# The low part of a weight a block later, a norm's squares four blocks later, its root behind the next splits

## The chip, the cores and the metric

One core of one Trainium2 chip runs the whole program. The metric is the device time of one execution in microseconds (us). TensorE (PE) does the matrix products and ScalarE (ACT), VectorE (DVE) and GpSimd (POOL) the rest. Each of them takes its instructions strictly in the order in which they were written for it, and an instruction that waits for a semaphore holds all that stand behind it. SyncE (SP) issues the transfers of the weights.

## The reference, cut to what matters

Two transformer blocks, each of depth 2, follow one another on 256 tokens of width 1024 (the first block carries 256 context tokens along in its first layer). Everything is float32. What matters here is the same everywhere: a residual stream `h`, an RMS norm of it, and a product of the normed stream with wide weights.

```python
def rms_norm(x, g, eps=NORM_EPS):              # first block
    xf = x.astype(jnp.float32)
    y = xf * lax.rsqrt(jnp.mean(xf * xf, axis=-1, keepdims=True) + eps)
    return (y * g.astype(jnp.float32)).astype(x.dtype)
...
    h_x = h_x + gt1 * y_x                                                # w_out
    f_x = modulate(rms_norm(h_x, g_ffn[l]), sh2, sc2)
    h_x = h_x + gt2 * conv_ffn(f_x, w_up[l], conv_w[l], conv_b[l], w_down[l])
    ...
    return rms_norm(h_x, g_final)
...
for layer in range(DEPTH):                     # second block
    h = h + 0.5 * _swiglu(_rmsnorm(h, ffn1_norm[layer]), ffn1_w_in[layer], ffn1_w_out[layer])
    hn = _rmsnorm(h, mix_norm[layer])
    if layer < N_A_LAYERS:
        h = h + _stick_breaking_mixer(hn, sb_w_qkv[layer], sb_w_out[layer])
    else:
        h = h + _nsa_mixer(hn, kvs, nsa_w_in[i], nsa_q_norm[i], nsa_w_out[i], cos, sin)
    h = h + 0.5 * _swiglu(_rmsnorm(h, ffn2_norm[layer]), ffn2_w_in[layer], ffn2_w_out[layer])
```

## The kernel before

**Splits.** A float32 weight is too precise for one pass of TensorE, so each is cut into a high and a low part, and each product is three matmuls: high by high, high by the activation's low part, low by high (L1207, L1208, L1209, and L1224, L1225, L1226 in the form described below). Weights come from memory in slabs of 2048 columns into three buffers RAWB. A slab is used in pieces of 1024 columns. A piece is split in two steps: ACT copies it, rounded, into WH (L1579), then DVE subtracts that from the raw weight into WL (L1899). There are four buffers for split pieces (`NW`), so the piece four ahead can be rounded only when the matmuls on a piece are done.

**Blocks.** The result is kept with its features on the 128 partitions, and a block is 128 output features. With 8 input tiles (`kt=8`) a block is 24 matmuls and uses one piece; in a down-projection chunk with 4 input tiles (`kt=4`) a block is 12 matmuls and a piece serves two blocks. Each block's bank is evacuated by DVE; in a residual stage (w_out, sb_out, nsa_out and the last chunk of each down projection) it is added into the stream H (L2098, L2128, L2132).

**The order.** One object, `Plan`, writes a single list of steps, and each engine's program walks that list and takes its own part of every step. Before a block's matmuls, `piece` calls `ahead`, which adds a `split` step for every free buffer; so the split of the piece three ahead stands on ACT and DVE just behind the evacuation of the block before.

**Norms behind a stage.** Nine residual stages feed a norm block by block (`hook`). Six use `EarlyNorm` (call them c1, f10, sb_out, f20, f11, nsa_out, in the order of time; c1, f10, f20 and f11 are last chunks of down projections, `kt=4`, the other two have `kt=8`). The norm's root is applied only to the results of the next stage, so the next stage's matmuls need just the stream itself, scaled by the gain and split: AH on ACT (L1607), AL on DVE (L1934). For the root each block is squared on ACT (L1619, L1620; the first also loads the table of Sqrt, L1613) into one of two SQ buffers, POOL adds it to an accumulator GT (L1145), TensorE sums over partitions with two matmuls (L1279, L1281), ACT takes the square root (L1628) and DVE the reciprocal (L1942). c1 is the widest: two norms in one, squares of 512 columns, and a longer chain behind the sum (L1944 to L1952). Three stages (the w_out of both layers and the last down chunk of layer 0) use `NormPlan`: there TensorE sums each block's squares and has to wait at the end for root (L1638), reciprocal (L1930), product (L1963) and the split of the normed stream (L1647, L1651, L1968).

**The next stage.** Its first two blocks run together (`mm_lead`, L1224 to L1226): for each of the eight input tiles six matmuls, 48 in all, so that tile 7 is needed last. The two sums of the norm stand behind them on TensorE.

Of the kernel before, what the change touches and what calls it, by code (L numbers as in the profile page):

```python
# [145 lines left out]
class Plan:  # L146


    def __init__(self, slabs):
        self.known, self.slabs, self.steps, self.put_off = slabs, [], [], []  # L150
        self.banks = Ring(self, 8)
        self.tmps, self.sqs, self.gts = Ring(self, 4), Ring(self, 2), Ring(self, 2)
# [70 lines left out]
    def ahead(self):  # L223
        while self.next_piece < len(self.pieces) and not self.held[self.next_piece % NW]:
# [4 lines left out]
            self.add("split", p=p)  # L229
            self.next_piece += 1  # L230

    def piece(self, s, i):
        if not self.known:
            return Piece(0, s, s.cuts[i])
        self.ahead()
        return self.pieces[s.first + i]
# [6 lines left out]
    def gemm(self, name, w, col0, ncols, T, src, ready, ev, kt=8, k0=0, width=256, fine=True, x=None, hook=None, lead=False):  # L243
        g = Gemm(name, kt, T, src, ready, ev, x)
        for c in range(0, ncols, width):
# [57 lines left out]
    def gemm_tok(self, name, w, col0, ncols, tiles, src, ready, ev, fine=True, x=None):  # L303
        g = Gemm(name, 8, 256, src, ready, ev, x)
# [288 lines left out]
    def ffn(self, name, w_up, w_down, T, ready, up, res, rx, hook):  # L593
        chunks = [[0, 1]] + [list(range(c, c + 4)) for c in range(2, 22, 4)]

        def do_up(ci):
            base = (ci % 2) * 4
# [33 lines left out]
        def do_down(ci, hook=None):  # L631
            kt = len(chunks[ci])
# [243 lines left out]
class NormPlan:  # L876
# [27 lines left out]
    def split(self, name, T, segs, W, a0=0):  # L904
        plan = self.plan
        self.sum()
        plan.mark("A" + name)
        plan.ahead()
# [16 lines left out]
class EarlyNorm:  # L925
# [4 lines left out]
    def __init__(self, plan, name, gain, first=None):  # L930
        self.plan, self.name, self.gain, self.first, self.n, self.low = plan, name, gain, first, 0, None

    def add(self, k, after):
        plan, i = self.plan, self.n
        self.n += 1
        if i == 0:
            plan.mark("A" + self.name)
            self.acc = plan.gts.take()
        q = plan.sqs.take() if i else None
        plan.add("xhi", (self.name, k), x=(after, self.gain))  # L940
# [4 lines left out]
        if self.low is not None:  # L945
            plan.add("xlow", (self.name, self.low), x=self.gain)
        self.low = k
        if i == 7:
            plan.add("xlow", (self.name, k), x=self.gain)
            b = plan.banks.take()  # L950
            plan.add("xroot", (self.name,), b=b, x=(plan.root_was, self.first))
            plan.later(1, lambda: self.sum(b, q))

    def sum(self, b, q):
        plan, name = self.plan, self.name
        plan.add("xsum", (name,), b=b, t=(self.acc, q), x=512 if self.first else 256)
        plan.sqs.give(q, ("xsum", name))
        plan.gts.give(self.acc, ("xsum", name))
        plan.banks.give(b, ("xroot", name))
# [1550 lines left out]
```

## Time and profile before

| | before |
|---|---|
| time, median of 3 runs | 2776.19 us (2770.31 to 2776.48) |
| the profiled execution: its own time | 2759.57 us |
| the profiled execution: its span | 2757.8 us |
| TensorE busy | 2562.5 us, 93% of the span |
| VectorE, ScalarE, GpSimd busy | 57%, 44%, 7% |
| mean granted TensorE clock | 0.974 of full speed |
| share of the chain that ended last | PE 77%, DVE 10%, ACT 8%, DMA 3% |

The profile shows one execution, and its time is 16.6 us under the median of the timed ones. A matmul's duration in it is modelled and overlaps the next one's; how fast TensorE goes is read from the distance between starts. A row of a timeline gives start, duration, engine, line, operation, what it writes and reads with the shapes, the count of merged instructions, and in brackets how long the engine had been idle and what ended that.

### The profile page before, as it was taken

What the parts mean: (1) busy time and instruction counts of PE and PEld (TensorE: products, weight loads), DVE (VectorE), ACT (ScalarE), POOL (GpSimd) and SP (SyncE); (2) the same over time, 40 slices, a digit from 0 to 9 for tenths busy, and PEclk for the clock granted to TensorE, in tenths of its full rate; (3) what the DMA queues carried; (4) which work ended last, traced back from release to release, by engine and by line L of the source; (5) the groups of instructions that cost most, each with busy time, mean ns of one, the idle gap of its engine ahead of it and who ended that gap; (6) DMA issues with size and microseconds to landing.
All of it is one profiled execution on the core that took longest, in us unless ns stands there. A gap on an engine that the chain in (4) does not pass through costs nothing.

```text
span 2757.8 us, 42208 instructions
## 1 busy us (share of the span) xinstructions
PE 2562.5 (93%) x17840; PEld 2259.0 (82%) x17840; DVE 1576.3 (57%) x2657; ACT 1219.8 (44%) x2025; POOL 187.4 (7%) x239
## 2 busy tenths in 40 slices
PE   5997899998999998999989989999799999988999
PEld 2875577776777776878889989998799999976999
DVE  2333234545565555364668877666566675766665
ACT  3224334424333324354556554445444553555543
POOL 0000000000000000000000011010010110025100
PEclk8998999999999999999999999999899999999999
DMA  7224432231454543233354546554265456530554
GB/s 243 67 86 131 134 105 84 67 99 61 136 169 138 168 131 129 85 115 101 122 168 155 190 145 207 185 168 130 71 201 190 153 191 199 168 126 16 169 197 140
DMA packets 337387, 382.12 MB, mean 139 GB/s; under 512 B 7408, under 2 KB 301296, under 8 KB 337200
## 3 DMA queue, kind: packets, MB, share of 16 engines
q1 hardware_dynamic: 334656, 370.37, 41.2%
q0 software_dynamic: 2544, 9.06, 1.1%
q8 instruction: 141, 2.31, 0.4%
q14 instruction: 46, 0.38, 0.0%
HBM read 378.36 MB, written 1.05 MB: 138 GB/s over the span
## 4 chain that ended last, share of the span: by engine, by line
PE 77%; DVE 10%; ACT 8%; DMA 3%; issue 2%; POOL 0%; SPq 0%; DVEq 0%; ACTq 0%; POOLq 0%
PE PS L1207 20%; PE PS L1209 19%; PE PS L1208 19%; DVE WL L1899 3%; ACT WH L1579 2%; PE PS L1242 1%; PE PS L1244 1%; PE PS L1243 1%; PE PS L1255 1%; PE PS L1224 1%; DMA RAWB<-in_w_in 1%; PE PS L1225 1%; PE PS L1226 1%; PE PS L1273 1%; PE PS L1340 1%
## 5 line engine op out<-in xcount | busy, mean ns | idle before, releaser
L1899 DVE TENSOR_TENSOR WL<-RAWB,WH 128x1024 fp32r<-128x1024 f32 (+2 forms) x613 | 734.7, 1206 | 650.5 <-ACT WH L1579 649.0
L1207 PE MATMUL PS<-AH,WH 128*128 128x256 f32 (+1 forms) x2912 | 910.7, 313 | 13.8 <-DVE WL L1899 13.8
L1209 PE MATMUL PS<-AH,WL 128*128 128x256 f32 (+1 forms) x2912 | 896.6, 308 | 0.0
L1208 PE MATMUL PS<-AL,WH 128*128 128x256 f32 (+1 forms) x2912 | 896.5, 308 | 0.0
L1579 ACT ACTIVATE WH<-RAWB 128x1024 fp32r<-128x1024 f32 (+2 forms) x613 | 625.3, 1033 | 320.0 <-PE PS L1209 167.1
L1207 PEld LDWEIGHTS PS<-AH,WH 128*128 128x128 f32 x2912 | 548.9, 189 | 70.1 <-issue 22.1
L1209 PEld LDWEIGHTS PS<-AH,WL 128*128 128x128 f32 x2912 | 548.7, 188 | 31.1
L1208 PEld LDWEIGHTS PS<-AL,WH 128*128 128x128 f32 x2912 | 548.5, 188 | 29.6 <-issue 0.5
L1207 PE MATMUL PS<-BH,WH 128*128 128x256 f32 (+1 forms) x1440 | 452.2, 314 | 0.8 <-DVE WL L1899 0.8
L1209 PE MATMUL PS<-BH,WL 128*128 128x256 f32 (+1 forms) x1440 | 439.2, 305 | 0.0
L1208 PE MATMUL PS<-BL,WH 128*128 128x256 f32 (+1 forms) x1440 | 438.5, 305 | 0.0
L1207 PEld LDWEIGHTS PS<-BH,WH 128*128 128x128 f32 x1440 | 271.5, 189 | 31.8 <-issue 13.9
L1208 PEld LDWEIGHTS PS<-BL,WH 128*128 128x128 f32 x1440 | 271.2, 188 | 15.7 <-issue 3.1
L1209 PEld LDWEIGHTS PS<-BH,WL 128*128 128x128 f32 x1440 | 271.2, 188 | 14.0
L1695 ACT ACTIVATE F<-PS,PV 128x512 f32<-128x512 f32 (+1 forms) x88 | 58.4, 666 | 136.5 <-PE PS L1209 131.0
L1224 PE MATMUL PS<-AH,WH 128*128 128x256 f32 (+1 forms) x160 | 58.0, 363 | 52.1 <-DVE AL L1968 17.2
L2105 DVE SCALAR_TENSOR_TENSOR F<-PS,PV,F 128x255 f32<-128x255 f32 x132 | 63.1, 478 | 68.6 <-ACT F L1695 68.4
L2098 DVE SCALAR_TENSOR_TENSOR H<-PS,MOD,H 128x256 f32<-128x256 f32 x168 | 72.8, 478 | 48.1 <-PE PS L1209 37.4
L1242 PE MATMUL PS<-WH,AH 128*128 128x256 f32 x352 | 99.0, 281 | 0.0
L1244 PE MATMUL PS<-WH,AL 128*128 128x256 f32 x352 | 98.1, 279 | 0.0
L1243 PE MATMUL PS<-WL,AH 128*128 128x256 f32 x352 | 98.1, 279 | 0.0
L1224 PEld LDWEIGHTS PS<-AH,WH 128*128 128x128 f32 x160 | 36.4, 227 | 60.1 <-DVE AL L1968 27.6
(314 smaller groups left out, 2827.9 us busy)
## 6 DMA issues: line engine op xcount, KB each, us to landing
RAWB<-in_f_in SPq DMA_DIRECT2D x88, 1024.0 KB, 5.2
RAWB<-in_w_in SPq DMA_DIRECT2D x52, 1024.0 KB, 5.1
RAWB<-in_w_ada SPq DMA_DIRECT2D x48, 1024.0 KB, 5.4
RAWB<-in_w_up SPq DMA_DIRECT2D x44, 1024.0 KB, 5.2
RAWB<-in_f_out SPq DMA_DIRECT2D x40, 1024.0 KB, 5.1
RAWB<-in_w_down SPq DMA_DIRECT2D x20, 1024.0 KB, 5.3
RAWB<-in_sb_qkv SPq DMA_DIRECT2D x12, 1024.0 KB, 5.4
RAWB<-in_w_out SPq DMA_DIRECT2D x8, 1024.0 KB, 5.1
```

The lines of the kernel that those rows point to most:

```text
L1207: pe.matmul(out, h, xh[:, 0:T], start=k == 0, stop=False)
L1208: pe.matmul(out, h, xl[:, 0:T], start=False, stop=False)
L1209: i = pe.matmul(out, l, xh[:, 0:T], start=False, stop=k == g.kt - 1)
L1224: pe.matmul(out[j], h, xh[:, 0:T], start=k == 0, stop=False)
L1242: pe.matmul(out, h, wh, start=k == 0, stop=False)
L1243: pe.matmul(out, h, wl, start=False, stop=False)
L1244: i = pe.matmul(out, l, wh, start=False, stop=k == 7)
L1579: act.activation(c.part("WH", p), c.raw(p.slab)[:, k0:k1, c0:c1], ACT.Copy).then_inc(up("hi", ("hi", p.p)), 1)
L1695: act.activation(c.wide(s.t, g), b[:, 0:T], ACT.Identity, bias=c.sm(f"conv_b{l}", n, 1), scale=c.sm(f"conv_w{l}", 44 + n, 1)).then_inc(up( ...
L1899: dve.tensor_tensor(c.part("WL", p), c.raw(p.slab)[:, k0:k1, c0:c1], c.part("WH", p).bitcast(F32), ALU.subtract).then_inc(up("lo", ("lo", ...
L2098: t = stt(x, b[:, q * 256:q * 256 + 256], c.mod(l, part, n, q), x, ALU.mult, ALU.add)
L2105: stt(x[:, a + 1:e], b[:, a:e - 1], c.sm(f"conv_w{l}", n, 1), x[:, a + 1:e], ALU.mult, ALU.add).then_inc(up("vec", ("upb", g.name, n, q)), 1)
```

## The change

Four things move; nothing is computed that was not computed before.

- The step `split` becomes two, `split_hi` for ACT and `split_lo` for DVE. In a stage with a hook (`lag` is set) the low part of a piece is ordered at the next call of `ahead`, a block or a pair of blocks later, unless the piece is needed at once. Everywhere else both stand together as before.
- In `EarlyNorm` the square of block i is ordered with block i+4, and the last ones follow the last block's low part.
- There the root (`xroot`) is ordered behind the sum, one tick into the next stage, and so behind the splits which that stage's first `ahead` adds. Its bank is taken there too.
- `NormPlan` itself is unchanged, but its stages set `lag`.

```diff
@@ Plan
     def ahead(self):
+
+        self.low_parts()
         while self.next_piece < len(self.pieces) and not self.held[self.next_piece % NW]:
             ...
             self.held[p.p % NW] = True
-            self.add("split", p=p)
+            self.add("split_hi", p=p)
+            self.rounded.append(p)
             self.next_piece += 1
+        if not self.lag:
+            self.low_parts()
+
+    def low_parts(self):
+        for p in self.rounded:
+            self.add("split_lo", p=p)
+        self.rounded = []

     def piece(self, s, i):
         ...
         self.ahead()
-        return self.pieces[s.first + i]
+        p = self.pieces[s.first + i]
+        if p in self.rounded:
+            self.low_parts()
+        return p
@@ gemm, do_down
+        self.lag = hook is not None
@@ gemm_tok, do_up, NormPlan.split
+        self.lag = False
@@ EarlyNorm.add (block k, the i-th)
-        q = plan.sqs.take() if i else None
         plan.add("xhi", (self.name, k), x=(after, self.gain))
-        plan.add("xsq", (self.name, i), n=k, b=self.acc, t=q, x=(after, self.first))
-        if 0 < i < 7:
-            plan.add("sqadd", ...)
-            plan.sqs.give(q, ("sqadd", self.name, i))
         if self.low is not None:
             plan.add("xlow", (self.name, self.low), x=self.gain)
         self.low = k
+        self.squares.append((i, k, after))
+        if i > 3:
+            self.square()
         if i == 7:
             plan.add("xlow", (self.name, k), x=self.gain)
-            b = plan.banks.take()
-            plan.add("xroot", (self.name,), b=b, x=(plan.root_was, self.first))
-            plan.later(1, lambda: self.sum(b, q))
+            while self.squares:
+                q = self.square()
+            plan.later(1, lambda was=plan.root_was: self.sum(q, was))
...
-    def sum(self, b, q):
+    def sum(self, q, was):
+        b = plan.banks.take()
         plan.add("xsum", (name,), b=b, t=(self.acc, q), x=512 if self.first else 256)
         ...
+        plan.add("xroot", (name,), b=b, x=(was, self.first))
```

`square` adds the steps `xsq` and `sqadd` for the oldest block in the list, as `add` did before.

Three places show what moves. On TensorE and GpSimd the order is the same but for bank numbers. The first place is VectorE in sb_out, blocks 2 to 5 (H is the residual add of a block, AL the low part of a stream tile, WL that of a weight piece); before:

```order
L2132 TENSOR_TENSOR H<-PS3,H 128x256
L1934 SCALAR_TENSOR_TENSOR AL<-H,PV,AH 128x256
L1899 TENSOR_TENSOR WL<-RAWB,WH 128x1024
L2132 TENSOR_TENSOR H<-PS4,H 128x256
L1934 SCALAR_TENSOR_TENSOR AL<-H,PV,AH 128x256
L1899 TENSOR_TENSOR WL<-RAWB,WH 128x1024
L2132 TENSOR_TENSOR H<-PS5,H 128x256
```

and now, at the same blocks:

```order
L2161 TENSOR_TENSOR H<-PS3,H 128x256
L1963 SCALAR_TENSOR_TENSOR AL<-H,PV,AH 128x256
L1928 TENSOR_TENSOR WL<-RAWB,WH 128x1024 x2
L2161 TENSOR_TENSOR H<-PS4,H 128x256
L1963 SCALAR_TENSOR_TENSOR AL<-H,PV,AH 128x256
L1928 TENSOR_TENSOR WL<-RAWB,WH 128x1024
L2161 TENSOR_TENSOR H<-PS5,H 128x256
```

The pattern looks the same, but the two pieces which stood ahead of block 2's add now stand behind it, and from there on each WL is that of the piece rounded one block earlier.

The second place is ScalarE at the end of sb_out and the start of the next stage (AH the high part of a stream tile, SQ a square, WH the high part of a weight piece, RS the root); before:

```order
L1579 ACTIVATE WH<-RAWB 128x1024
L1607 ACTIVATE AH<-H,PV 128x256
L1620 ACTIVATE SQ<-H 128x256
L1628 ACTIVATE RS<-PS1,EPS 128x256
L1579 ACTIVATE WH<-RAWB 128x1024
L1699 ACT_TABLE_LOAD
```

and now:

```order
L1608 ACTIVATE WH<-RAWB 128x1024
L1636 ACTIVATE AH<-H,PV 128x256
L1649 ACTIVATE SQ<-H 128x256 x5
L1608 ACTIVATE WH<-RAWB 128x1024
L1657 ACTIVATE RS<-PS3,EPS 128x256
L1728 ACT_TABLE_LOAD
```

Four more squares stand behind the last AH, and the root stands behind the next piece's WH instead of ahead of it.

The third place is VectorE behind the w_out of layer 0, a `NormPlan` stage (RS the reciprocal of the root, TMP the normed stream); before:

```order
L1899 TENSOR_TENSOR WL<-RAWB,WH 128x1024
L2098 SCALAR_TENSOR_TENSOR H<-PS2,MOD,H 128x256 x2
L1930 RECIPROCAL RS<-RS 128x512
L1899 TENSOR_TENSOR WL<-RAWB,WH 128x1024
L1963 SCALAR_TENSOR_TENSOR TMP<-H,G2,RS 128x256 x6
```

and now:

```order
L1928 TENSOR_TENSOR WL<-RAWB,WH 128x1024
L2127 SCALAR_TENSOR_TENSOR H<-PS2,MOD,H 128x256 x2
L1959 RECIPROCAL RS<-RS 128x512
L1928 TENSOR_TENSOR WL<-RAWB,WH 128x1024 x2
L1992 SCALAR_TENSOR_TENSOR TMP<-H,G2,RS 128x256 x6
```

Two low parts now stand between the reciprocal and the first product, where one stood.

## Rows read from the trace of the kernel before

**Rows 1.** Page, engines: busy us, share of the span, instructions.

```profile
PE 2562.5 (93%) x17840; PEld 2259.0 (82%) x17840; DVE 1576.3 (57%) x2657; ACT 1219.8 (44%) x2025; POOL 187.4 (7%) x239
```

**Rows 2.** Waits of TensorE, whole span: us in total, times, longest.

```profile
PE PS L1224 <- ACT TMP L1647: 16.9, 2, 8.4
PE PS L1207 <- DVE WL L1899: 14.7, 14, 4.5
PE PS L1224 <- DVE WL L1899: 13.1, 6, 3.7
```

**Rows 3.** Chain of waits in sb_out, one round: start us, us, what.

```profile
1980.12 1.23 DVE WL L1899
1981.35 0.34 DVE H L2132
...
1981.72 0.51 ACT AH L1607
1982.23 0.30 ACT SQ L1620
1982.53 0.95 ACT WH L1579
...
1983.51 1.24 DVE WL L1899
```

**Rows 4.** Timeline of TensorE, end of sb_out (two rows) and of nsa_out.

```profile
1980.95 0.28 PE L1209 MATMUL PS<-BH,WL 128*128 128x256 f32 x1
1984.88 0.55 PE L1224 MATMUL PS<-AH,WH 128*128 128x256 f32 x1 [3.65 <-DVE WL L1899]
...
2569.56 0.36 PE L1224 MATMUL PS<-AH,WH 128*128 128x256 f32 x1 [3.23 <-DVE WL L1899]
```

**Rows 5.** Stretches of TensorE: us, busy (x instructions), granted clock, DMA, GB/s.

```profile
1984.80:1990.80 6.00, 5.92 (x28) 0.50 0.52 175
2569.50:2575.00 5.50, 5.44 (x46) 1.00 0.58 191
```

**Rows 6.** Timeline of TensorE: behind the root after sb_out.

```profile
1997.79 0.39 PE L1207 MATMUL PS<-AH,WH 128*128 128x256 f32 x1 [0.61 <-DVE WL L1899]
2001.23 0.38 PE L1207 MATMUL PS<-AH,WH 128*128 128x256 f32 x1 [0.34 <-DVE WL L1899]
```

**Rows 7.** Timeline of TensorE after f20; the last row after f11.

```profile
2177.69 0.36 PE L1224 MATMUL PS<-AH,WH 128*128 128x256 f32 x1 [0.94 <-DVE WL L1899]
2182.45 0.39 PE L1224 MATMUL PS<-AH,WH 128*128 128x256 f32 x1 [0.99 <-DVE AL L1934]
2189.59 0.39 PE L1207 MATMUL PS<-AH,WH 128*128 128x256 f32 x1 [0.87 <-DVE WL L1899]
...
2444.55 0.48 PE L1459 MATMUL PS<-SQ,CC 128*128 128x256 f32 x1 [4.34 <-ACT SQ L1828]
```

**Rows 8.** Timeline of TensorE after c1.

```profile
1636.75 0.55 PE L1224 MATMUL PS<-AH,WH 128*128 128x256 f32 x1 [3.42 <-DVE WL L1899]
1646.28 1.02 PE L1279 MATMUL PS<-GT,CC 128*128 128x512 f32 x2
1655.35 0.58 PE L1207 MATMUL PS<-AH,WH 128*128 128x256 f32 x1 [4.47 <-DVE WL L1899]
```

**Rows 9.** Timeline of VectorE: the split behind c1's root, two rows behind w_out's reciprocal.

```profile
1654.08 1.22 DVE L1899 TENSOR_TENSOR WL<-RAWB,WH 128x1024 fp32r<-128x1024 f32 x1
...
666.11 1.16 DVE L1899 TENSOR_TENSOR WL<-RAWB,WH 128x1024 fp32r<-128x1024 f32 x1
667.19 2.45 DVE L1963 SCALAR_TENSOR_TENSOR TMP<-H,G,RS 128x256 f32<-128x256 f32 x6
```

**Rows 10.** Groups of POOL's adds, then two adds under VectorE's work.

```profile
L1145 POOL TENSOR_TENSOR GT<-GT,SQ 128x256 f32<-128x256 f32 x30 | 22.6, 753 | 251.3 <-ACT SQ L1620 250.4
L1145 POOL TENSOR_TENSOR GT<-GT,SQ 128x512 f32<-128x512 f32 x6 | 7.7, 1282 | 189.0 <-ACT SQ L1620 188.7
...
1837.76 1.68 POOL L1145 TENSOR_TENSOR GT<-GT,SQ 128x256 f32<-128x256 f32 x2 [2.46 <-ACT SQ L1620]
```

More of the change, by code:

```diff
@@ L151, in __init__ @@
         self.banks = Ring(self, 8)
+        self.rounded, self.lag = [], False
         self.tmps, self.sqs, self.gts = Ring(self, 4), Ring(self, 2), Ring(self, 2)
@@ L596, in do_up @@
         def do_up(ci):
+            self.lag = False
             base = (ci % 2) * 4
@@ L631, in do_down @@
         def do_down(ci, hook=None):
+            self.lag = hook is not None
             kt = len(chunks[ci])
@@ L907, in split @@
         plan.mark("A" + name)
+        plan.lag = False
         plan.ahead()
@@ L931, in __init__ @@
         self.plan, self.name, self.gain, self.first, self.n, self.low = plan, name, gain, first, 0, None
+        self.squares = []
     def add(self, k, after):
@@ L938, in add, with square @@
             self.acc = plan.gts.take()
+        plan.add("xhi", (self.name, k), x=(after, self.gain))
+        if self.low is not None:
+            plan.add("xlow", (self.name, self.low), x=self.gain)
+        self.low = k
+        self.squares.append((i, k, after))
+        if i > 3:
+            self.square()
+        if i == 7:
+            plan.add("xlow", (self.name, k), x=self.gain)
+            while self.squares:
+                q = self.square()
+            plan.later(1, lambda was=plan.root_was: self.sum(q, was))
+    def square(self):
+        plan, (i, k, after) = self.plan, self.squares.pop(0)
         q = plan.sqs.take() if i else None
-        plan.add("xhi", (self.name, k), x=(after, self.gain))
         plan.add("xsq", (self.name, i), n=k, b=self.acc, t=q, x=(after, self.first))
@@ L944, in add @@
             plan.sqs.give(q, ("sqadd", self.name, i))
[L945 to L949, printed above, removed]
-            b = plan.banks.take()
-            plan.add("xroot", (self.name,), b=b, x=(plan.root_was, self.first))
-            plan.later(1, lambda: self.sum(b, q))
-    def sum(self, b, q):
+        return q
+    def sum(self, q, was):
         plan, name = self.plan, self.name
+        b = plan.banks.take()
         plan.add("xsum", (name,), b=b, t=(self.acc, q), x=512 if self.first else 256)
@@ L1572, in scalar_program @@
             c.ev.when[("mark", "act", id)] = (m["sem"]["acted"], c.ev.count.get("acted", 0))
-        elif kind == "split":
+        elif kind == "split_hi":
             p = s.p
@@ L1894, in vector_program @@
             c.ev.when[("mark", "dve", id)] = (m["sem"]["vec"], c.ev.count.get("vec", 0))
-        elif kind == "split":
+        elif kind == "split_lo":
             p = s.p
```

## The prediction

> **What bounds the kernel now.** I read the engines' busy shares first, then TensorE's waits, then the chain of waits inside the stages that the change touches, and last the timelines at the ends of those stages. TensorE is busy for 93% of the span [rows 1], so a reordering on VectorE and ScalarE can only give back the idle time at places where TensorE waits for them, and the clock that such idle time costs. The waits name low parts of weights, WL on VectorE, in both forms of the matmul: 13.1 us over 6 waits of the leading blocks and 14.7 us over 14 others; the 16.9 us for TMP are two waits of 8.4 behind a `NormPlan` norm [rows 2].
>
> The chain shows why WL is late. In sb_out it doesn't run over TensorE at all. It goes round in a loop: WL, then the residual add H behind it on VectorE, then AH, SQ and WH in ScalarE's order, then the next WL, which waits for that WH [rows 3]. The round takes from 1980.12 to 1983.51, 3.39 us, while a block of 24 matmuls at the full rate takes 24 x 0.12 = 2.9 (5.50 us for 46 of them, 0.12 each [rows 5]). So the splits lose about half a microsecond per block against TensorE, eat up the three pieces of lead, and at the end TensorE stands: 3.65 us before the leading blocks of the next stage, 3.23 after nsa_out [rows 4]. After the first of them the clock was granted at 0.50, the 1.2 GHz level, for 28 matmuls in 6.00 us; after the second it stayed at 1.00 [rows 5].
>
> **The loop is opened.** The low part of a piece now stands a block behind its high part, and the squares of the first four blocks leave the stage's first half. A WL then waits for a WH that was ordered a block earlier and is long done. What is left per block is throughput. On VectorE 0.34 for H, 0.4 for AL and 1.23 for WL, 2.0 us; on ScalarE 0.51 + 0.30 + 0.95 = 1.8 us [rows 3], with AL set a little above an H. Both are under 2.9. With a piece per two blocks (the down projections) it is 0.34 + 0.4 twice and 1.23 once, 2.7 us on VectorE per 2.9 us of TensorE: just enough, and it starts from a lead of three pieces. I walked the new order through the last four blocks with these durations: the second leading piece's WL ends 0.7 us ahead of its use after sb_out and about as much after the f stages. So the wait ahead of the leading blocks goes in all six stages.
>
> Terms, stage by stage (0.16 is added to an idle time where a matmul's modelled 0.28 hides a step of 0.12):
> - sb_out: 3.65 + 0.16 = 3.8 [rows 4]; the half clock, 6.00 us for 28 matmuls that take 28 x 0.12 = 3.35 at full clock, 2.65 [rows 5]; and the two waits behind the root, 0.61 + 0.34, about 0.95 [rows 6], since that WL is no longer behind the reciprocal. Sum 7.4.
> - nsa_out: 3.23 + 0.16 = 3.4 [rows 4]; no half clock there [rows 5]; 0.95 behind the root, taken from sb_out as the next stage is of the same form [rows 6]. Sum 4.3.
> - f20: 0.94 + 0.99 + 0.87, each with 0.16, 3.3, and a few tenths of a later wait [rows 7]. f10 has the same form; f11 has the first of these waits, and then TensorE waits 4.34 us for squares of the next stage's result, which need the root [rows 7]. Taking one WL of 1.23 [rows 3] from ahead of its consumer there gives some 0.7, since that WL now may delay the reciprocal by half its own length. I take 3.0, 3.5 and 2.4, sum 9.
> - c1: before, 3.42 us ahead of the leading blocks, then half a clock, then 4.47 us for the WL that stands behind the whole root chain [rows 8, 9]. Now that WL is done early, but the next pieces can only be rounded behind the first Silu, which needs the root. The two sums on TensorE need POOL's last add; c1's adds take 1.28 us each [rows 10] and four of them (blocks 3 to 6) follow the last block, with squares of some 0.7 us (two instructions, an SQ being 0.30 [rows 3]) handing over two buffers. By this walk the last add ends 9.6 us after the stage's last matmul, 3.9 after the leading blocks. Root and next piece follow as before: from the sums at 1646.28 to the WL at 1654.08 and from there some 3.5 to the piece after it [rows 8, 9]. That puts the third block behind the leading ones 20.9 us after the stage, against 27.2 now (last matmul 1633.05, which is 1636.75 less 3.42 and 0.28; the third block at 1655.35 plus 24 matmuls at the half clock, 1660.3 [rows 8]). So 6.3 is gained at most; with one more stretch of half clock behind the new wait, 2.65 less, 3.7. I take 5.
>
> Sum of gains: 7.4 + 4.3 + 9 + 5 = 25.7 us.
>
> **What it costs.** Behind the three `NormPlan` stages the late WL comes to stand with the next one between the reciprocal and the first product. TensorE has nothing to do there (8.4 us of waiting [rows 2]), so every instruction put in is paid in full: 1.08 us from the start of WL to the product behind it [rows 9]. Three times 1.1 is 3.3 us. Nothing hides it. From below the bound is zero, if the WL found room elsewhere, which the order excludes; from above each could draw out the half clock by a stretch worth 2.65 [rows 5], 3.75 each, 11.3 in all. I take 3.3, for the restart is only a little later than now. The table load is moved from block 0 to block 4 and costs ScalarE the same there; the transfers wait for a low part a block later, 2.9 us, of the two slabs, some 11 us, that they run ahead. Both I set at nothing; if the transfers had less cover, it would be a wait of ScalarE at WH.
>
> The squares are the other debt. Behind the last block ScalarE has five of them and POOL four adds. An add takes 0.75, and 0.84 where two follow each other [rows 10], so in the five stages with 256 columns they end some 5.6 us after the last block; the leading blocks take 48 x 0.12 = 5.7. They just fit: cost nothing, with no margin.
>
> The Trainium skill's page "GPSIMD Engine Reference", section "Specifications", says that GpSimd shares its SBUF interfaces with VectorE and that they contend when a VectorE instruction has two SBUF inputs, as WL and AL have. The trace shows a little of it: 0.84 per add while VectorE works on AL and WL, against 0.75 on the mean [rows 10]. If the rule bit harder here, with all adds under AL and WL, the sums would come later, which is the first rival below.
>
> **The sum.** 25.7 less 3.3 is 22.4 us: the profiled execution's 2759.6 would become 2737. The timed runs' median lies 16.6 us above it, and I take the difference over unchanged: 2776.2 - 22.4 = 2754 us.
>
> **Rivals.**
> 1. The sums become the wait. If the chain of squares and adds behind the last block is 1 to 2 us longer than walked (slower hand-overs between ScalarE and POOL, slower adds), TensorE stands ahead of its two sums in five stages, about 1.5 each, and c1 gives nothing more than its leading wait, 3.4 instead of 5; one half clock comes back, 2.65. That takes 7.5 + 1.6 + 2.65 from 22.4 and leaves 10.6: 2766 us. For it: no margin. Against it: adds have followed each other at 0.84.
> 2. The same chain goes fully serial, square, add, square, add, and the kernel becomes slower. A step is then 0.4 + 0.84 and two hand-overs of 0.1, 1.4 us; five steps and the way to the first put the sums some 3.5 us behind the leading blocks, each with a half clock of 2.65: 6.2 in five stages. In c1 a step is 0.7 + 1.28 + 0.2, and it is 7 + 2.65 late. 41 us in all, against 22.4: 2795. It decides the sign from a lateness of 3.7 us per stage (22.4 over six). Against it: there are two buffers, so only every second square waits.
> 3. The change doesn't do what it says: the splits stay late, because VectorE's 2.7 us per 2.9 in a down projection leaves nothing to catch up, and sb_out and nsa_out win what NormPlan and c1 lose. Then the f stages keep their waits (9), c1 gives 0, no half clock is saved: 22.4 - 9 - 5 - 2.65 = 5.8, 2770 us, hardly to be told from no change.
>
> **Chances.** The forecast 0.70, with a range of its own from 2743 to 2762 (c1 between 0 and 6.3, the clock of sb_out saved or not, NormPlan up to 11.3). Rival 1 has 0.16, rival 2 has 0.05, rival 3 has 0.09. A measurement here can tell 0.3%, 8.3 us. Faster than that holds the forecast and most of rival 1 (0.70 + 0.13), and some of rival 3 (0.02): 0.85. Rivals 2 and a little of 3 are slower: 0.06. The rest, 0.09, is no change. The range reaches from 2740, where c1 gives its most and two more half clocks vanish, to 2769.
>
> **What would show it.** In the profile after: in sb_out and nsa_out the adds H should follow each block's last matmul instead of a WL, 2.9 us apart or a little less, instead of 3.39; TensorE's waits for WL in both forms should fall from 27.8 us to under 8, most of it left after c1. The stretch at 0.50 after sb_out should be gone. TensorE's waits for TMP should rise by 1.1 each. In c1 a new wait of TensorE should stand ahead of L1279's successor for GT or SQ, about 4 us; in the other five none over 0.5. The forecast is wrong if those sums wait over 1 us in the five stages, if H still starts right behind WL, or if the leading blocks still wait for WL.

## The result and the profile after

In runs on the same chip the kernel before took 2773.5 us (median of 18) and the changed one 2757.0 (18 runs, 2747.1 to 2769.2). The ratio is 0.9944, 95% interval 0.9933 to 0.9956: 16 us faster, where 22.4 were forecast. The forecast time, 2754, was off by 3.0 us; it was built on a median of 2776.2 for the kernel before, which with 18 runs is 2773.5. The profiled execution took 2750.2 us with a span of 2748.4.

TensorE's waits of the kernel after, whole span, answer to [rows 2] (us in total, times, longest):

```profile
PE PS L1253 <- ACT TMP L1676: 19.2, 2, 9.6
PE PS L1253 <- DVE AL L1997: 18.4, 2, 11.9
...
PE PS L1236 <- DVE WL L1928: 10.0, 11, 3.4
```

The leading blocks (L1253 now) no longer wait for WL at all, and the other matmuls (L1236) wait 10.0 us for it instead of 14.7. TMP has risen by 1.1 us per wait (8.45 to 9.58 in the timelines). The residual adds in sb_out, from VectorE's timeline, answer to [rows 3]:

```profile
1970.31 0.42 DVE L2161 TENSOR_TENSOR H<-PS,H 128x256 f32<-128x256 f32 x1 [0.70 <-PE PS L1238]
...
1973.13 0.42 DVE L2161 TENSOR_TENSOR H<-PS,H 128x256 f32<-128x256 f32 x1 [0.87 <-PE PS L1238]
...
1975.96 0.42 DVE L2161 TENSOR_TENSOR H<-PS,H 128x256 f32<-128x256 f32 x1 [0.65 <-PE PS L1238]
...
1978.79 0.42 DVE L2161 TENSOR_TENSOR H<-PS,H 128x256 f32<-128x256 f32 x1 [0.87 <-PE PS L1238]
```

They come 2.83 us apart, where it was 3.39 before, and wait for the matmuls and no longer for a WL. The timeline of TensorE, in the order of time, answers to [rows 4, 6 to 8] and, by its first row, to the waits of `NormPlan`:

```profile
668.08 0.77 PE L1253 MATMUL PS<-AH,WH 128*128 128x512 f32 x1 [9.58 <-ACT TMP L1676]
...
1647.70 2.08 PE L1308 MATMUL PS<-GT,CC 128*128 128x512 f32 x2 [4.96 <-POOL GT L1174]
...
1661.16 0.39 PE L1236 MATMUL PS<-AH,WH 128*128 128x256 f32 x1 [3.40 <-DVE WL L1928]
...
1843.89 0.70 PE L1308 MATMUL PS<-GT,CC 128*128 128x256 f32 x2 [0.94 <-POOL GT L1174]
...
1984.38 0.70 PE L1308 MATMUL PS<-GT,CC 128*128 128x256 f32 x2
...
1991.52 0.38 PE L1236 MATMUL PS<-AH,WH 128*128 128x256 f32 x1 [0.35 <-DVE WL L1928]
...
2173.89 0.70 PE L1308 MATMUL PS<-GT,CC 128*128 128x256 f32 x2 [1.20 <-POOL GT L1174]
...
2431.32 1.22 PE L1488 MATMUL PS<-SQ,CC 128*128 128x256 f32 x2 [3.39 <-ACT SQ L1857]
```

After sb_out TensorE now runs into its two sums without a wait (the row without brackets). A new wait has come up: for POOL's last add, 4.96 us after c1, 0.94 after f10 and 1.20 after f20. The clock of two stretches, of TensorE's windows, answers to [rows 5]:

```profile
1645.50:1652.30 6.80, 4.60 (x9) 0.53 0.42 128
1978.60:1990.00 11.40, 11.40 (x94) 1.00 0.52 171
```

Behind sb_out the granted clock stays at 1.00, 2.4 GHz. Behind c1 it falls to about a half after TensorE has stood for POOL. Why it stands is in POOL's timeline: c1, then f10, sb_out, f20 and f11:

```profile
1639.89 7.75 POOL L1174 TENSOR_TENSOR GT<-GT,SQ 128x512 f32<-128x512 f32 x5 [0.76 <-ACT SQ L1649]
...
1838.77 5.06 POOL L1174 TENSOR_TENSOR GT<-GT,SQ 128x256 f32<-128x256 f32 x5 [0.91 <-ACT SQ L1649]
...
1974.83 1.07 POOL L1174 TENSOR_TENSOR GT<-GT,SQ 128x256 f32<-128x256 f32 x1 [131.00 <-ACT SQ L1649]
...
1980.14 4.19 POOL L1174 TENSOR_TENSOR GT<-GT,SQ 128x256 f32<-128x256 f32 x4 [1.63 <-ACT SQ L1649]
...
2168.51 5.32 POOL L1174 TENSOR_TENSOR GT<-GT,SQ 128x256 f32<-128x256 f32 x5 [0.91 <-ACT SQ L1649]
...
2422.34 4.41 POOL L1174 TENSOR_TENSOR GT<-GT,SQ 128x256 f32<-128x256 f32 x5 [0.38 <-ACT SQ L1649]
```

In c1 five adds take 7.75 us, 1.55 each, where 1.28 was expected. In sb_out four small ones take 4.19, 1.05 each instead of 0.84 [rows 10]. The means hide what happens: one add of each group is long, 2.06 us in c1 (it starts at 1642.77), 1.54 in f10 (1840.54) and sb_out (1981.02), 1.81 in f20 (2170.28), and each of these stands beside a WL. The others take 1.26 to 1.30 and 0.72 to 0.74, with 0.14 between one and the next. In f11 the longest takes 0.87. And behind f10, f20 and f11 five adds follow each other and not four.

**Where the time went.** One distance sums up each place: from the start of a stage's last matmul to that of the first matmul of the third block behind the leading ones (for f10, to the two transposes just ahead of it; for f11, to the matmul behind TensorE's wait for the squares, L1459 before and L1488 after). Each is a difference of two starts in a timeline, like 1991.52 less 1978.47 for sb_out. The last columns are the sum and the timed difference to before (ratio less 1, times 2772 us; its interval is 6 to 18 us wide). L covers the three `NormPlan` stages too where nothing else is said.

| kernel (L low parts, S squares, R root moved) | c1 | f10 | f20 | f11 | sb_out | nsa_out | sum | timed |
|---|---|---|---|---|---|---|---|---|
| before | 27.2 | 15.8 | 16.5 | 13.0 | 20.3 | 17.2 | 110.0 | |
| before, second profile | 27.2 | 15.8 | 16.5 | 13.4 | 19.8 | 18.5 | 111.2 | -1.1 |
| after: L, S, R | 24.4 | 13.5 | 14.3 | 10.2 | 13.0 | 13.0 | 88.4 | -15.5 |
| after, second profile | 24.4 | 13.5 | 14.5 | 10.2 | 13.0 | 13.0 | 88.6 | -18.3 |
| L, S, R, not for NormPlan | 24.3 | 13.5 | 14.3 | 10.2 | 13.1 | 13.1 | 88.4 | -19.7 |
| L | 28.8 | 19.4 | 18.7 | 12.5 | 17.5 | 17.5 | 114.4 | +5.0 |
| R | 24.8 | 14.7 | 15.4 | 12.0 | 17.9 | 17.9 | 102.8 | -5.3 |
| S, R | 28.6 | 18.2 | 18.2 | 13.8 | 17.4 | 17.4 | 113.7 | -1.7 |
| L, S | 28.7 | 18.7 | 19.0 | 11.6 | 17.5 | 17.3 | 112.7 | +6.1 |
| L, R, not for NormPlan | 22.7 | 13.1 | 13.8 | 11.2 | 12.6 | 12.8 | 86.2 | -22.5 |
| L, R, not for NormPlan, squares 2 later in c1 | 20.5 | 13.1 | 13.8 | 11.2 | 12.8 | 12.8 | 84.2 | -20.8 |
| L, R, not for NormPlan, squares 2 later | 20.5 | 13.1 | 13.8 | 11.2 | 12.8 | 12.8 | 84.2 | -23.6 |
| L, R, not for NormPlan, lag by stage | 20.5 | 13.3 | 14.3 | 11.4 | 12.8 | 12.8 | 85.2 | -19.4 |
| L, R, not for NormPlan, tiny adds | 18.5 | 12.3 | 12.8 | 10.2 | 12.8 | 12.8 | 79.4 | -34.4 |

The changed kernel gains 21.5 us at the six places (before rounding) and loses 1.13 at each of three NormPlan norms: 18.1, near the 16 us timed. The two profiles alone differ by only 9.4; the last section says why. In the other rows, too, the sums less that of before, with 3.4 added where L covers `NormPlan`, lie within 3 us of the timed difference in most and within 6 in all; S, R is furthest off (3.8 us slower by the sum, 1.7 faster as timed).

### The profile page after: what moved, and what is told of

It is laid out like the page before. It is cut to its first block, busy times and chain, and to the rows that moved or that the text cites. A ratio compares the mean times of both kernels' runs of the same rounds, so it can differ in the third digit from the quotient of the medians.

```text
span 2748.4 us, 42207 instructions
## 1 busy us (share of the span) xinstructions
PE 2569.6 (93%) x17840; PEld 2265.6 (82%) x17840; DVE 1578.8 (57%) x2657; ACT 1222.3 (44%) x2025; POOL 193.0 (7%) x239
## 3 DMA queue, kind: packets, MB, share of 16 engines
HBM read 378.36 MB, written 1.05 MB: 138 GB/s over the span
## 4 chain that ended last, share of the span: by engine, by line
PE 80%; DVE 9%; ACT 6%; DMA 3%; issue 1%; POOL 1%; SPq 0%; POOLq 0%; ACTq 0%; DVEq 0%
PE PS L1236 21%; PE PS L1238 20%; PE PS L1237 20%; DVE WL L1928 2%; ACT WH L1608 2%; PE PS L1271 1%; PE PS L1273 1%; PE PS L1272 1%; PE PS L1284 1%; DMA RAWB<-in_w_in 1%; PE PS L1302 1%; POOL GT L1174 1%; PE PS L1253 1%; PE PS L1369 1%; PE PS L1254 1%
## 5 line engine op out<-in xcount | busy, mean ns | idle before, releaser
L1236 PE MATMUL PS<-AH,WH 128*128 128x256 f32 (+1 forms) x2912 | 912.1, 313 | 9.2 <-DVE WL L1928 9.2
L1236 PEld LDWEIGHTS PS<-AH,WH 128*128 128x128 f32 x2912 | 548.9, 189 | 66.0 <-issue 21.2
L1236 PE MATMUL PS<-BH,WH 128*128 128x256 f32 (+1 forms) x1440 | 452.2, 314 | 0.8 <-DVE WL L1928 0.8
L1236 PEld LDWEIGHTS PS<-BH,WH 128*128 128x128 f32 x1440 | 271.0, 188 | 31.8 <-issue 13.9
L1237 PEld LDWEIGHTS PS<-BL,WH 128*128 128x128 f32 x1440 | 271.2, 188 | 15.4 <-issue 3.1
L1253 PE MATMUL PS<-AH,WH 128*128 128x256 f32 (+1 forms) x160 | 54.0, 337 | 39.8 <-ACT TMP L1676 19.2
L2157 DVE SCALAR_TENSOR_TENSOR H<-PS,H 128x256 f32<-128x256 f32 x192 | 77.5, 419 | 20.2 <-PE PS L1238 19.0
```

The costliest lines, as they stand in the source:

```text
L1236: pe.matmul(out, h, xh[:, 0:T], start=k == 0, stop=False)
L1237: pe.matmul(out, h, xl[:, 0:T], start=False, stop=False)
L1253: pe.matmul(out[j], h, xh[:, 0:T], start=k == 0, stop=False)
L2157: stt(x, b[:, 0:256], 0.5, x, ALU.mult, ALU.add).then_inc(up("vec", ("ev", g.name, n)), 1)
```

## The experiments

**Both kernels again** (`e4_before_again`, `e8_after_again`): unchanged copies, for second profiles.

> The kernel before itself, for a second profile. The profiles of before and after differ by 9.4 us, the medians by 16.5. Theory A: the rest lies in stretches that the change does not touch: behind nsa_out before made 1238 matmuls in 140 us and after 1191, both at a granted clock of 1.00, some 6 us by the end; if that is a state of one execution, a second profile of before shows some 1190 matmuls there, and a span 6 to 15 us longer. Theory B: it belongs to the change (what the moved instructions do to the stages behind them); then this profile again shows 1238 in 140 us. On the clock: either its runs have a mean granted clock of 0.973 or more where the changed kernel's have 0.966 to 0.972 (the change costs clock), or they spread over the same values.

> The changed kernel itself on the same chip as these, with a second profile. Its time should be 13 to 19 us under before again. If the waits are the change's own, they are the same to a tenth of a microsecond (TMP 9.6, GT 5.0 after c1, 0.9 to 1.2 after f10 and f20), while the stretches at 0.50 away from the six stages (747.8, 1249.6, 2201.9, 2335.0, 2430.6, 2464.7, 2492.0 and 2522.7 in the first profile) move or are missing if they belong to the single execution.

Measured: before again 0.9996 (0.9983 to 1.0009), after again 0.9934 (0.9908 to 0.9959), 18 us under before. The waits at the places of the change came back in the second profiles, most of them to within 0.1 us (TMP 9.6, GT 5.0 after c1 and 0.94 after f10; before, 3.22 after nsa_out, where the first has 3.23). Three did not: in the kernel after, the wait for POOL after f20 is 1.63 and not 1.20, and in the kernel before, the waits ahead of the leading blocks are 3.23 and not 3.65 after sb_out and 1.36 and not 0.94 after f11. All eight stretches at 0.50 that the expectation lists came back, 3 to 6 us later, so they belong to the kernel and not to the single execution. The mean granted clock of the single executions was 0.966 to 0.973 after and 0.965 to 0.975 before, so the change costs no clock that these runs can tell.

**The low parts alone** (`e1_low_only`). Squares and root go back to their places:

```diff
-        if i > 3:
-            self.square()
+        q = self.square()
...
-            plan.later(1, lambda was=plan.root_was: self.sum(q, was))
+            b = plan.banks.take()
+            plan.add("xroot", (self.name,), b=b, x=(plan.root_was, self.first))
+            plan.later(1, lambda: self.sum(q, b))
```

> The changed kernel with its squares and its root back in their old places: only the low parts of the weights are ordered a block later. Theory A (the loop WL, H, AH, SQ, WH, WL was the loss, and the late low part alone opens it): ScalarE has 0.51 + 0.30 + 0.95 = 1.8 us per block of 2.9 even with the squares in it, so the adds H in sb_out still follow the matmuls 2.9 us apart or less, no wait for WL ahead of the leading blocks, and the sums of the five stages with 256 columns wait under 0.3 us. The time is within 3 us of the changed kernel's: 13 to 19 us under before. In c1, where a pair of blocks needs 2 x (0.51 + 0.9) + 1.04 = 3.9 us of ScalarE against 2.83 of TensorE, there is a new wait ahead of the leading blocks of about 1 to 3 us, but none of 5 us ahead of the sums. Theory B (the squares' move opened the loop): the adds stay 3.2 to 3.4 us apart and the time is within 5 us of before.

Measured: 1.0018 (1.0002 to 1.0034), 5 us slower than before. The adds H do come 2.83 us apart (1985.65, 1988.47, 1991.30 in its timeline) and nothing waits ahead of the leading blocks of sb_out, as theory A said (0.64 is left there in the f stages and 2.74 in c1), yet all of the gain is gone. Its timeline behind sb_out, all engines but the weight loads:

```profile
1999.58 0.59 PE L1307 MATMUL PS<-GT,CC 128*128 128x256 f32 x2
2000.01 0.59 PE L1309 MATMUL PS<-SQ,CC 128*128 128x256 f32 x2
2000.64 0.47 ACT L1656 ACTIVATE RS<-PS,EPS 128x256 f32<-128x256 f32 x1 [5.24 <-PE PS L1309]
2001.02 1.05 ACT L1607 ACTIVATE WH<-RAWB 128x1024 fp32r<-128x1024 f32 x1
2001.15 1.75 DVE L1970 RECIPROCAL RS<-RS 128x256 f32<-128x256 f32 x1 [5.54 <-ACT RS L1656]
2002.08 1.28 ACT L1727 ACT_TABLE_LOAD   x1
2002.82 2.29 DVE L1927 TENSOR_TENSOR WL<-RAWB,WH 128x1024 fp32r<-128x1024 f32 x2
2004.04 0.50 PE L1235 MATMUL PS<-AH,WH 128*128 128x256 f32 x1 [3.43 <-DVE WL L1927]
```

The sums come at once, 5.8 us behind the stage. But ScalarE has been idle for 5.24 us, since the root stands ahead of the next WH, and both WLs stand behind the reciprocal. TensorE waits 3.43 us there. The same wait, 3.43, stands after f10 and nsa_out, and after c1 it is 7.2. Before the change, the wait ahead of the leading blocks had covered most of it: 0.61 + 0.34 was all that showed behind the root [rows 6].

**The root alone** (`e9_root_only`): the changed kernel with `self.lag = False` everywhere and `q = self.square()` in place of the squares' lag.

> The kernel before with one part of the change: the root behind the next stage's splits. Low parts and squares stay in their old places. Theory C (root and low part need each other: with the root early, WL waits behind it; with WL late, TensorE waits ahead of the leading blocks): the wait ahead of the leading blocks stays (3.4 to 3.7 us after sb_out and nsa_out, 0.9 after f10 and f20), the waits of 0.6 and 0.3 behind the root go; the third block behind the leading ones comes some 1 us earlier in sb_out and nsa_out and up to 1 in the others. 2 to 7 us under before, ratio 0.9975 to 0.9993. Rival G (the root's place alone is the gain): third block after sb_out at 13 to 15 us behind the stage instead of 20, more than 12 us under before.

Measured: 0.9981 (0.9966 to 0.9996), 5 us faster, as theory C said. In TensorE's timeline the lead wait stays (3.34 after sb_out), and behind the root 0.35 is left:

```profile
1990.03 0.35 PE L1252 MATMUL PS<-AH,WH 128*128 128x256 f32 x1 [3.34 <-DVE WL L1927]
...
2004.31 0.39 PE L1235 MATMUL PS<-AH,WH 128*128 128x256 f32 x1 [0.35 <-DVE WL L1927]
```

**The change less its root** (`e5_root_old_place`): the second half of the diff above, on the changed kernel.

> The changed kernel with one part taken back: the root stands ahead of the next stage's splits again; low parts a block later and squares four blocks later stay. Theory C (found in the run with the low parts alone: there TensorE no longer waited ahead of the leading blocks or the sums, but 3.43 us for WL behind each root, 7.2 after c1, since WH stands behind the root on ScalarE): the same wait of 3.4 us comes back in all six stages, on top of the waits of about 1 us for the sums, and the time is within 5 us of before, 2767 to 2777 against 2772. Theory D (the prediction's account, the root's place is worth 0.95 us per stage): 4 to 6 us above the changed kernel, some 11 us under before.

Measured: 1.0022 (1.0005 to 1.0038). Theory D, which is the prediction's account of the root, falls: taking it back costs some 22 us and not 4 to 6. TensorE's waits of this kernel:

```profile
PE PS L1236 <- DVE WL L1928: 26.0, 10, 7.2
...
PE PS L1308 <- POOL GT L1174: 4.5, 2, 4.4
```

**The change less its low parts** (`e2_squares_root_only`): `self.lag = False` everywhere.

> The changed kernel with every low part ordered right behind its high part, as before: only the squares (four blocks later) and the root (behind the next splits) are moved. Theory A: a round of the loop loses only the square's 0.30 of 3.39 us in its first four blocks, and has it back in the last four; the wait ahead of the leading blocks after sb_out stays at 2 to 3.5 us, and what is gained is the wait behind the root, about 1 us in four stages: 3 to 9 us under before, NormPlan's waits for TMP unchanged at 8.4. Theory B (the squares' move opened the loop): adds 2.9 us apart, 13 us or more under before.

Measured: 0.9994 (0.9979 to 1.0009), no difference; theory A had 3 to 9 us. Squares moved without the low parts do harm, seen against the root alone (113.7 against 102.8 in the table). The wait ahead of the leading blocks after sb_out is 2.17 us, as theory A said, but inside the leading blocks there is a longer one than before: 3.51 in c1 and 1.42 in f10, where it was 0.74 and 0.99. There, in TensorE's timeline after c1, they wait for an AL: ScalarE has the table load of Sqrt (1.28 us) and squares ahead of the last WH, and WL, H and AL come behind that. Then TensorE waits for POOL:

```profile
1635.70 0.39 PE L1253 MATMUL PS<-AH,WH 128*128 128x256 f32 x1 [3.51 <-DVE AL L1963]
...
1643.56 2.08 PE L1308 MATMUL PS<-GT,CC 128*128 128x512 f32 x2 [3.71 <-POOL GT L1174]
```

**NormPlan's stages as before** (`e3_no_lag_for_normplan`):

```diff
-        self.lag = hook is not None
+        self.lag = isinstance(hook, EarlyNorm)
```

> The changed kernel, but the three stages behind which a NormPlan norm stands keep their low parts where they were before. Theory A: the late low part costs there what the profile of the changed kernel shows against before, 1.9 + 1.15 + 0.65 = 3.7 us: TMP waits fall from 9.6 back to about 8.4, the time is 3 to 4 us below the changed kernel's, 19 to 21 us under before. Rival: the cost there is partly another draw of the half clock, and the late low part also saved something inside these stages: within 1.5 us of the changed kernel.

Measured: 0.9929 (0.9912 to 0.9945). That is 4 us below the first comparison of the changed kernel and 1 below the second, and the intervals overlap: the times alone don't show it. The profile does, at the norm behind w_out:

```profile
668.01 0.76 PE L1253 MATMUL PS<-AH,WH 128*128 128x512 f32 x1 [8.45 <-ACT TMP L1676]
```

9.58 is 8.45 again: 1.13 us per norm, 3.4 in all.

**Every square with its own block** (`e6_squares_at_once`): the edit for NormPlan, and `q = self.square()`.

> Low parts a block later in the six EarlyNorm stages alone (NormPlan's left as before), root behind the next splits, but every square ordered with its own block. Theory E (the squares' lag is needed for nothing in the five stages with 256 columns: ScalarE has 1.8 us of work per 2.9, POOL 1.2): the waits of 0.5 to 1.2 us for POOL ahead of the sums are gone there, each of the five gains about 1 us over the kernel without the lag for NormPlan; in c1 ScalarE needs 3.9 us per pair of blocks against 2.83, so TensorE waits about 2 to 3 us ahead of the leading blocks and then not for POOL (5.0 in the changed kernel). Sum 4 to 7 us under that kernel, 24 to 28 under before, ratio 0.990 to 0.9915. Rival F (the squares in the stage delay WH, and the splits are late again): a wait for WL of over 1 us ahead of the leading blocks in each stage, no better than the changed kernel.

Measured: 0.9919 (0.9897 to 0.9940), 22.5 us under before. The waits for POOL are gone; sb_out and nsa_out gain 0.2 to 0.5 each over a lag of four, not 1. But f10, f20 and f11 have a wait of about 0.75 us ahead of their leading blocks again, and c1 one of 3.65. Only c1 is over the 1 us that rival F named as its mark.

**Two blocks later** in c1 alone (`e7_c1_two_blocks_later`) and everywhere (`e10_two_blocks_later`): `while len(self.squares) > 2: q = self.square()`.

> As the kernel with every square at its own block, but in c1 the squares come two blocks later. Theory E: c1's debt of ScalarE (2 x 1.3 + 1.04 = 3.6 us per pair of 2.83) is then paid while the leading blocks run: the wait ahead of them is under 1 us, the one ahead of the sums 0 to 3 us, and the time is 1 to 3 us under the kernel with lag 0 in c1. Against it: POOL's adds of 1.3 to 1.55 us, two per pair of blocks, are then still a block and a half behind, and c1 gains nothing.

> Low parts a block later in the six EarlyNorm stages alone, root behind the next splits, squares two blocks later in all six instead of four. Theory E (a lag of four leaves POOL a debt of four adds, which under VectorE's work take 1.0 us and more and not the 0.84 of my walk; a lag of none puts the table load and the squares ahead of the last splits): with two, the wait ahead of the leading blocks in f10, f20 and f11 is gone (0.9 with lag 0) and the one ahead of the sums too (0.8 to 1.2 with lag 4); third block behind the leading ones at about 12.5 us in f10, 13.2 in f20, 12.8 after sb_out and nsa_out, 20.5 in c1. 4 to 6 us under the changed kernel without the lag for NormPlan; ratio to before 0.989 to 0.992. Rival F: the debt of ScalarE alone delays the next WH, the same 13.0 and 13.8 as with lag 0.

Measured: 0.9925 (0.9903 to 0.9946) and 0.9915 (0.9890 to 0.9939). The profiles show c1 2.2 us shorter than with no lag; what is left there are waits of 1.1 us ahead of the leading blocks and 1.6 to 1.8 for POOL. The times can't tell it. In the f stages a lag of two changes nothing: 13.1 and 13.8, as rival F said, and theory E falls there.

**A lag for each stage** (`e11_lag_by_stage`): none in sb_out and nsa_out, two in c1, three in the f stages.

> Low parts a block later in the six EarlyNorm stages alone, root behind the next splits, and the squares' lag chosen by stage: none in sb_out and nsa_out, two blocks in c1, three in f10, f20 and f11. With lags of none and two these three stages wait 0.7 to 1.0 us ahead of the leading blocks, with four 0.8 to 1.2 ahead of the sums (none in f11). Theory H (POOL's adds slow the WLs beside them from 1.23 to 1.77 us; with three blocks of lag only one or two stand inside the stage): both waits under 0.5 us, third block at 12.6 us in f10 and 13.4 in f20, 10.3 in f11; 1 to 2 us under the kernel with two blocks everywhere, ratio to before 0.988 to 0.992. Against it: no difference that shows, since what one wait loses the other takes.

Measured: 0.9930 (0.9908 to 0.9953). A miss: the lead wait was 0.99 us after f10, not under 0.5, and the sum of distances 85.2, worse than 84.2. In f10 the table load now stands between two AH, the AL behind it waits 0.92 us (at 1830.51 on VectorE), and the last WL still takes 1.77.

**Tiny adds** (`e12_small_adds`), on `e6_squares_at_once`. Each add of POOL takes 4 columns; the rest of the sum of squares is left out:

```diff
-            acc = c.gt(s.b)[:, 0:s.x]
+            acc = c.gt(s.b)[:, 0:4]
...
-            pool.tensor_tensor(acc, acc, c.sq(s.t)[:, 0:s.x], ALU.add)...
+            pool.tensor_tensor(acc, acc, c.sq(s.t)[:, 0:4], ALU.add)...
```

> The kernel with every square at its own block (low part a block later, root behind the splits, NormPlan's stages as before), but each of POOL's adds takes 4 columns instead of 256 or 512: the rest of the sum of squares is left out. Order, waits and all work of VectorE and ScalarE stay. Theory H (POOL and VectorE slow each other: adds 1.13 us on the mean here against 0.74 where no split stands beside them, WL 1.77 against 1.23): every WL in f10's last blocks takes 1.22 to 1.23, and the wait of 0.7 to 1.0 us ahead of the leading blocks after f10, f20 and f11 is gone; c1's wait there (3.7 us, ScalarE's work) shrinks by under 1.5. Theory I (the squares on ScalarE, not POOL's adds, make the last splits late): WL again 1.77 or the wait again 0.7 to 1.0.

Measured: 0.9876 (0.9843 to 0.9908). The six distances give 6.8 us of the 12 to `e6_squares_at_once`; its six runs spread over 28 us, so the rest says little. Same order, same work on VectorE and ScalarE. Timelines of VectorE in the last blocks of f10, first with whole adds:

```profile
1830.03 1.76 DVE L1927 TENSOR_TENSOR WL<-RAWB,WH 128x1024 fp32r<-128x1024 f32 x1
1831.71 0.41 DVE L2156 SCALAR_TENSOR_TENSOR H<-PS,H 128x256 f32<-128x256 f32 x1
1832.05 0.61 DVE L1962 SCALAR_TENSOR_TENSOR AL<-H,PV,AH 128x256 fp32r<-128x256 f32 x1
```

then with tiny ones:

```profile
1828.60 1.21 DVE L1927 TENSOR_TENSOR WL<-RAWB,WH 128x1024 fp32r<-128x1024 f32 x1
1829.74 0.41 DVE L2156 SCALAR_TENSOR_TENSOR H<-PS,H 128x256 f32<-128x256 f32 x1
1830.07 0.47 DVE L1962 SCALAR_TENSOR_TENSOR AL<-H,PV,AH 128x256 fp32r<-128x256 f32 x1
```

WL is back from 1.76 to 1.21 us, and the wait ahead of the leading blocks of all three f stages is gone. In f10 and c1 ScalarE had not waited for POOL with whole adds either, so it is VectorE's longer instructions that had made the last splits late. Theory H holds. It was too small in c1: the wait there fell from 3.65 to 0.93, not by under 1.5, so most of it was POOL's doing and not ScalarE's. With whole adds two AL there had taken 1.13 and 1.09 us instead of 0.48, and the last WL 2.29 instead of 1.22.

## Why the prediction was right, and where not

- **The loop.** Right: adds 2.83 us apart, no wait for WL ahead of the leading blocks in any of the six, no half clock after sb_out. One sign was missed: the waits for WL fell from 27.8 to 10.0 us and not under 8, and 3.4 of them stand after c1.
- **sb_out and nsa_out.** 7.4 and 4.3 forecast, 7.2 and 4.1 measured between the two first profiles. The sum was right and its split was wrong. The step "the two waits behind the root, 0.61 + 0.34, about 0.95" gives the root's place the price of the wait that the trace of before shows. That trace had the root's delay mostly hidden behind a longer one; with the low parts alone moved it is 3.43 us in three of the six stages and 7.2 in c1. Neither part has most of the gain. By the six distances, which leave NormPlan's cost out, the low parts alone are 4.4 us worse than before, the root alone 7.1 better, both together 23.8 better; timed, +5.0 (with NormPlan's 3.4 in it), -5.3 and -22.5. The forecast came out because both were in it, and in that it was lucky.
- **The f stages.** 3.0, 3.5 and 2.4 forecast, 2.3, 2.2 and 2.8 measured. The failed step is "they just fit: cost nothing, with no margin". It counts four adds of 0.84. Behind f10 and f20 five adds follow each other, in 5.06 and 5.32 us, and one of them, beside a WL, takes 1.54 and 1.81. So the sums waited 0.94 and 1.20 us there, over the 0.5 named as the sign. Either alone costs nothing: f11 has five adds but none over 0.87, sb_out and nsa_out have one of 1.54 but four adds, and none of the three has a wait. That was rival 1's mechanism (slower adds), in two of its five stages. The 0.84 was also misread as "while VectorE works on AL and WL": those two adds start at 1837.76 and end at 1839.44 [rows 10], with an AL beside the first, and the next WL begins only at 1839.39 in VectorE's timeline. No row that the prediction shows prices an add under a WL.
- **c1.** 5 forecast, 2.9 measured, the term that was off most. The third block came 24.35 us after the stage and not 20.9. The last add was 1.2 us late of the walk (10.8 us after the stage instead of 9.6), 0.8 of it by the add of 2.06 us beside a WL; the two sums then ran at half clock (2.8 us to the next block instead of 1.3). The rest, 0.7, lies in the chain from the root to the next WL, where the walk was short: it gave "some 3.5" from one WL to the piece after it, which before is 1657.39 less 1654.08 and a split of 1.2, 4.5.
- **NormPlan.** 3.3 forecast, 3.4 measured. The table load, set at nothing, costs nothing in the changed kernel; with the squares moved alone, and with a lag of three, it stands ahead of splits that TensorE waits for.
- **Sum.** 25.7 less 3.3 forecast, 21.5 less 3.4 measured. The terms of c1 and the f stages make 3.7 of the 4.3 us by which the two nets differ. The forecast time looks better than the forecast gain (22.4 against 16 timed) because the median of before came out 2.7 us lower with more runs; that part is luck.
- **The squares' lag** was called part of what opens the loop ("the squares of the first four blocks leave the stage's first half"). It wasn't needed: with none the times are no worse (0.9919 against 0.9929 with a lag of four, overlapping) and the six distances 2.2 us shorter.

The versions without NormPlan's lag and with squares two blocks later or at once are 0.9915 and 0.9919 of before, against 0.9944 and 0.9934 for the changed kernel. The profiles put them 5.6 to 7.6 us ahead of it; the intervals of the times overlap.

## What to carry to other kernels

When one queue feeds several consumers in turn, the wait that a trace shows can hide those behind it. Price a reordering as a set: walk the new order through all later waits. Parts that are worth little alone can be worth the whole sum together, as they were here. An engine that is 7% busy is not free to add work to, if its work holds up the engine that the bound hangs on.

## What the runs showed of the hardware

**GpSimd and VectorE make each other wait.** Groups of POOL's adds (instructions, busy us, mean ns). Low parts in their old places, squares moved, so that hardly a split stands beside them:

```profile
L1174 POOL TENSOR_TENSOR GT<-GT,SQ 128x256 f32<-128x256 f32 x30 | 22.1, 738 | 269.3 <-ACT SQ L1649 266.8
```

The kernel after:

```profile
L1174 POOL TENSOR_TENSOR GT<-GT,SQ 128x256 f32<-128x256 f32 x30 | 27.4, 912 | 242.1 <-ACT SQ L1649 239.5
```

Low parts a block later and squares at once, so that nearly all adds stand beside a WL:

```profile
L1173 POOL TENSOR_TENSOR GT<-GT,SQ 128x256 f32<-128x256 f32 x30 | 33.9, 1129 | 219.0 <-ACT SQ L1648 218.1
```

The same instruction takes 738, 912 or 1129 ns on the mean by what VectorE does, and WL takes up to 1.76 us instead of 1.21. The residual add H, which reads one tile from PSUM, stays at 0.41. The Trainium skill's "GPSIMD Engine Reference", section "Specifications", says that the two contend for SBUF interfaces when a VectorE instruction has two SBUF inputs; WL has two. By that rule the trace agrees.

The means are mixtures. In the kernel after, the 17 small adds without a WL beside them take 0.74, the 13 with one 0.73 to 1.81. A WL and the add that begins inside it, behind sb_out:

```profile
1980.19 1.77 DVE L1928 TENSOR_TENSOR WL<-RAWB,WH 128x1024 fp32r<-128x1024 f32 x1
1981.02 1.54 POOL L1174 TENSOR_TENSOR GT<-GT,SQ 128x256 f32<-128x256 f32 x1
```

The WL begins 0.05 us after another add (1980.14, 0.74) and ends 1.08 after that add's end; alone it takes 1.22. The add that begins inside the WL ends 0.60 after the WL's end. The tiny adds of f10 show it most plainly, first one alone, then one that begins 0.62 us into the WL of 1828.60 shown above:

```profile
1824.30 0.20 POOL L1173 TENSOR_TENSOR GT<-GT,SQ 128x4 f32<-128x4 f32 x1 [19.92 <-ACT SQ L1648]
...
1829.22 0.66 POOL L1173 TENSOR_TENSOR GT<-GT,SQ 128x4 f32<-128x4 f32 x1 [0.48 <-ACT SQ L1648]
```

It ends at 1829.88, 0.07 us after the WL, and the WL keeps its 1.21. So in these rows the two don't both run at a lower rate: whichever comes second stands until the first is done, and the trace counts the standing as its duration. One add caught inside a WL costs POOL 0.8 us (1.54 instead of 0.74), one WL caught behind an add costs VectorE 0.55 (1.76 instead of 1.21).

**Two speeds of TensorE at one granted clock.** Window of 140 us in the last stage: before, first profile; before, second; after, first; after, second:

```profile
2600.00:2740.00 140.00, 140.00 (x1238) 1.00 0.60 196
```

```profile
2600.00:2740.00 140.00, 140.00 (x1191) 1.00 0.58 192
```

```profile
2600.00:2740.00 140.00, 140.00 (x1191) 1.00 0.51 167
```

```profile
2600.00:2740.00 140.00, 140.00 (x1238) 1.00 0.54 178
```

Both kernels show 0.113 us per matmul in one execution and 0.118 in another, 4% apart, with the clock granted at 1.00 both times. It isn't a matter of missing records: over the whole spans the distances between the starts of such matmuls fall in two groups, 0.113 to 0.114 and 0.117 to 0.119 us, with few between. The pace lasts for whole stages and changes from one execution to the next; it doesn't follow the DMA's rate (192 to 196 GB/s in one pair, 167 to 178 in the other). What sets it stays open.

From nsa_out's last matmul to the end, the first profile of before takes 191.7 us, mostly at the quicker pace, and the second 199.7, with one half clock more. That is 8 of the 12.3 us between the two spans, and a part, not all, of why the first lay 16.6 us under the median. The first profile of after has the slower pace there and takes 194.2: its nsa_out is 4.1 us shorter, but the pace gives 6.6 back. With these 6.6 the first two profiles would differ by 16.0 us instead of 9.4 (an estimate from these numbers), as the times do. For reading: compare distances at the places of a change, not spans.
